# Sparse attention and mLSTM layer: all eight heads' probabilities times values in one change of the matrix array's tiling, with six split weight slots instead of seven

## What is computed

```
h = rmsnorm(x) @ w_in           -> a_q a_k a_v a_z i_q i_k i_w b_q b_k b_v b_z b_o b_i b_f g_a g_b
score = sum over 16 index heads of w_i * relu(q_i . k_i / 8);  keep the best 128 admissible keys
logits = q_a . k_a / 8, masked to those keys;  p = softmax(logits)       # 8 heads of 64
o_a    = p @ v_a                                                         # 8 heads of 64
y_a    = (o_a * silu(a_z)) @ w_branch_a
y_b    = (head_norm(sigmoid(b_o) * mlstm(silu(conv(b_q, b_k)), b_v, gates)) * silu(b_z)) @ w_branch_b
out    = rmsnorm(x + (sigmoid(g_a) * y_a + sigmoid(g_b) * y_b) @ w_out)
```

## Time and profile before

| | us |
|---|---|
| median of three runs | 511.49 |
| the three runs | 511.46 to 511.62 |
| the profiled execution | 511.43 |
| its span, first to last instruction | 509.7 |
| PE busy | 500.9 |
| DVE busy | 258.7 |
| ACT busy | 236.1 |
| POOL busy | 214.6 |

### The profile page before, as it was taken

The page is one execution under the profiler, slowest core; times in us unless marked ns, Lnnn a source line. Parts: engine busy times, 40 slices in busy tenths (PEclk is TensorE's granted clock), DMA queues, the critical chain, the costliest instruction groups (busy, mean ns, idle before and its releaser), DMA issues.

```text
span 509.7 us, 6792 instructions
## 1 busy us (share of the span) xinstructions
PE 500.9 (98%) x2506; PEld 411.4 (81%) x2506; DVE 258.7 (51%) x568; ACT 236.1 (46%) x417; POOL 214.6 (42%) x142
## 2 busy tenths in 40 slices
PE   8999999999999999999999999999999999999995
PEld 7688888888888878888777877888888888887885
DVE  3875778877999915515555557551110011125433
ACT  6756754655533443464577563333321333142322
POOL 1675231333344453256487433056435653373000
PEclk9999999999999999999999999999999999999999
DMA  8653531222243432112121121142244326444111
GB/s 285 200 140 121 140 96 53 84 83 53 74 123 83 120 108 83 42 43 83 44 81 46 47 76 42 42 123 73 56 121 123 107 59 206 125 134 155 41 52 74
DMA packets 44842, 48.94 MB, mean 96 GB/s; under 512 B 4997, under 2 KB 30213, under 8 KB 44809
## 3 DMA queue, kind: packets, MB, share of 16 engines
q1 hardware_dynamic: 43944, 47.65, 32.0%
q10 hardware_dynamic: 864, 0.86, 0.5%
HBM read 46.40 MB, written 2.11 MB: 95 GB/s over the span
## 4 chain that ended last, share of the span: by engine, by line
PE 94%; DMA 2%; SPq 1%; POOL 1%; ACT 1%; DVE 1%; issue 1%; DVEq 0%
PE pj L1423 24%; PE pj L1425 23%; PE pj L1424 23%; PE ob L1533 2%; PE tr L1524 2%; DMA w_raw<-in_w_in 2%; PE ob L1504 2%; PE qb L1494 2%; PE qb L1489 2%; PE qb L1488 2%; PE ob L1424 1%; PE qb L1424 1%; PE ob L1425 1%; PE qb L1425 1%; PE ob L1423 1%; PE qb L1423 1%
## 5 line engine op out<-in xcount | busy, mean ns | idle before, releaser
L513 POOL TENSOR_TENSOR w_lo<-w_raw,w_hi 128x1024 fp32r<-128x1024 f32 x70 | 168.8, 2421 | 144.5 <-ACT w_hi L856 144.4
L1423 PE MATMUL pj<-w_hi,h_hi 128*128 128x512 f32 x272 | 112.8, 415 | 0.0
L1425 PE MATMUL pj<-w_hi,h_lo 128*128 128x512 f32 x272 | 106.5, 392 | 0.0
L1424 PE MATMUL pj<-w_lo,h_hi 128*128 128x512 f32 x272 | 106.5, 391 | 0.0
L1423 PE MATMUL pj<-h_hi,w_hi 128*128 128x512 f32 (+1 forms) x200 | 78.1, 390 | 1.0 <-DVE h_lo L1086 1.0
L856 ACT ACTIVATE w_hi<-w_raw 128x1024 fp32r<-128x1024 f32 (+1 forms) x72 | 73.5, 1045 | 10.2 <-DMA w_raw<-in_w_out 6.4
L1425 PE MATMUL pj<-h_hi,w_lo 128*128 128x512 f32 (+1 forms) x200 | 77.9, 389 | 0.0
L1424 PE MATMUL pj<-h_lo,w_hi 128*128 128x512 f32 (+1 forms) x200 | 77.9, 389 | 0.0
L1425 PEld LDWEIGHTS pj<-w_hi,h_lo 128*128 128x128 f32 x272 | 51.0, 188 | 11.4
L1423 PEld LDWEIGHTS pj<-w_hi,h_hi 128*128 128x128 f32 x272 | 51.2, 188 | 9.7 <-issue 1.1
L1424 PEld LDWEIGHTS pj<-w_lo,h_hi 128*128 128x128 f32 x272 | 51.3, 188 | 9.4 <-issue 1.0
(11 more groups left out here) (201 smaller groups left out, 817.6 us busy)
## 6 DMA issues: line engine op xcount, KB each, us to landing
w_raw<-in_w_in SPq DMA_DIRECT2D x60, 512.0 KB, 3.6
w_raw<-in_w_out SPq DMA_DIRECT2D x5, 512.0 KB, 3.7
x_tok<-in_x SPq DMA_DIRECT2D x4, 512.0 KB, 5.0
w_raw<-in_w_branch_a SPq DMA_DIRECT2D x8, 256.0 KB, 3.0
w_raw<-in_w_branch_b SPq DMA_DIRECT2D x8, 256.0 KB, 3.3
x_again<-in_x SPq DMA_DIRECT2D x1, 2048.0 KB, 10.4
w_late<-in_w_out SPq DMA_DIRECT2D x3, 512.0 KB, 7.3
out<-y_norm SPq DMA_DIRECT2D x4, 320.0 KB, 2.5
```

The source lines that it names most:

```text
L513: eng.tensor_tensor(lo[:, 0:m], raw_slot(n)[:, 0:m], hi[:, 0:m].bitcast(F32), ALU.subtract).then_inc(lo_by_dve if n in DVE_SLOTS else lo_b ...
L1423: pe.matmul(bank, a_hi, b_hi, start=first, stop=False)
L1424: pe.matmul(bank, a_hi, b_lo, start=False, stop=False)
L1425: return pe.matmul(bank, a_lo, b_hi, start=False, stop=last)
```

## The change

`pv_a` is now done once for each token tile, for all eight heads in a row, at attention places 10, 18, 26 and 34, which are the places where the last two heads of each tile were done before. That takes transposed probabilities of eight heads instead of two, in two pieces of four heads (`probs_t0`, `probs_t1`). Their space comes from the weight ring, `SPLIT` 6 instead of 7, and from `gated`, which moves to the zone of the queries `q_a`. With six places the third slot of the next group can no longer be made before the last unit, so `unit_slots` makes the third and the fourth both behind quarter 1 of the last unit. Three of the last eight slots go to places of their own (`EXTRA`) instead of one. `q_a` gets another layout, so that its tiles are contiguous.

```diff
-SPLIT = 7
+EXTRA = (LAST_PLACE, OUT0 + 3, OUT0 + 7)
+SPLIT = 6
...
-        if p >= 4 and p % 2 == 0:
-            put(q, "pv_a", p // 2 - 2)
+        if p >= 6 and p % A_HEADS == 2:
+            put(q, "pv_a", p // A_HEADS - 1)
...
+        z_p = zone(8192)
...
-        q_a = at("q_a", [P, KW, SEQ], F32, z_e)
+        q_a = at("q_a", [P, TILES, KW, P], F32, z_e)
...
-        probs_t = at("probs_t", [P, 2, SEQ], F32, z_h + 4096)
-        gated = at("gated", [P, 2, WIDTH], F32, z_h + 8192)
+        probs_t = [at(f"probs_t{n}", [P, A_HEADS // 2, SEQ], F32, place) for n, place in enumerate((z_h + 4096, z_p))]
+        gated = at("gated", [P, 2, WIDTH], F32, z_e)
...
-            if n == LAST_PLACE:
-                return SPLIT
-            return (n - OUT0 + GATE0 + 6 - (n > LAST_PLACE)) % SPLIT
+            if n in EXTRA:
+                return SPLIT + EXTRA.index(n)
+            return (n - OUT0 + GATE0 - (n > EXTRA[1])) % SPLIT
...
             if g in ("iq0", "iq1"):
-                return {3: [n, n + 1], 2: [n + 2], 1: [n + 3]}[j]
+                return {3: [n, n + 1], 2: [], 1: [n + 2, n + 3]}[j]
             if g == "az":
-                return [n + j] if j < 3 else []
-            return [n + j]
+                return ([n], [n + 1], [], [n + 2])[j]
+            return ([n], [n + 1], [], [n + 2, n + 3])[j]
...
-            return 1 if u + 1 < len(UNITS) and UNITS[u + 1][0] != UNITS[u][0] else -1
+            return 1 if u + 1 == len(UNITS) or UNITS[u + 1][0] != UNITS[u][0] else -1
...
-                    if s >= 2:
-                        wait_full(dve, ("pv_a", s // 2 - 1))
-                    dve.tensor_copy(probs_t[:, s % 2, 0:w], bank_of(job)[:, 0:w]).then_inc(probs_t_made, 1)
+                    if s >= A_HEADS:
+                        wait_full(dve, ("pv_a", s // A_HEADS - 1))
+                    dve.tensor_copy(turned(s % A_HEADS)[:, 0:w], bank_of(job)[:, 0:w]).then_inc(probs_t_made, 1)
...
-                    wait_read(pe, ("probs_chan", s + 1))
-                    b = h // 2
-                    for j in range(i + 1):
-                        for e in range(2):
+                    wait_read(pe, ("probs_chan", s + A_HEADS - 1))
+                    for d in range(0, A_HEADS, 2):
+                        b = (h + d) // 2
+                        for j in range(i + 1):
+                            for e in range(2):
```

More of the change, by code:

```diff
@@ L176, in fills @@
         ring = RING_OF[job[0]]
-        if job[0] == "pv_a" and ATTN[2 * job[1]][1]:
+        if job[0] == "pv_a" and ATTN[A_HEADS * job[1]][1]:
             bank[job] = bank[("pv_a", job[1] - 1)]
@@ L362, in hybrid_kernel @@
         final_row = at("final_row", [P, D_MODEL], F32, z_a + 8192)
-        w_last = [at("w_last_hi", [P, SLOT], F32R, z_f), at("w_last_lo", [P, SLOT], F32R, z_f + 4096)]
+        w_extra = [[at(f"w_extra{n}_{part}", [P, SLOT], F32R, place + size) for part, size in (("hi", 0), ("lo", 4096))]
+                   for n, place in enumerate((z_f, z_p, z_e))]
         y_tok = at("y_tok", [P, 2, D_MODEL], F32, z_hlo)
@@ L573, in wait_unit_read, with turned @@
                 eng.wait_ge(unit_out, u + 1)
+        def turned(head):
+            return probs_t[head // (A_HEADS // 2)][:, head % (A_HEADS // 2), :]
         def wait_slot_used(eng, n):
@@ L745, in side @@
                         hi = q_twice[same, i % 2, e, :, :]
-                        pool.tensor_tensor(q_lo[same, i % 2, e, :, :], q_a[same, :, i * P:(i + 1) * P],
+                        pool.tensor_tensor(q_lo[same, i % 2, e, :, :], q_a[same, i, :, :],
                                            hi.bitcast(F32), ALU.subtract).then_inc(q_lo_made, 1)
@@ L884, in job_side @@
                     wait_full(act, job)
[L885 removed]
+                    act.activation(q_a[:, j, :, :],
                                    bank_of(job)[:, :].rearrange("p (b t) -> p b t", t=P), ACT.Copy)\
@@ L981, in split_queries @@
                     same = slice(e * A_DIM, (e + 1) * A_DIM)
-                    act.activation(q_twice[same, i % 2, e, :, :], q_a[same, :, i * P:(i + 1) * P], ACT.Copy)\
+                    act.activation(q_twice[same, i % 2, e, :, :], q_a[same, i, :, :], ACT.Copy)\
                         .then_inc(q_hi_made, 1)
@@ L985, in split_queries @@
                     same, other = slice(e * A_DIM, (e + 1) * A_DIM), slice((1 - e) * A_DIM, (2 - e) * A_DIM)
-                    act.activation(q_twice[other, i % 2, e, :, :], q_a[same, :, i * P:(i + 1) * P], ACT.Copy)\
+                    act.activation(q_twice[other, i % 2, e, :, :], q_a[same, i, :, :], ACT.Copy)\
                         .then_inc(q_doubled, 1)
@@ L1525, in side @@
                 elif kind == "pv_a":
[L1526 removed]
+                    s = A_HEADS * job[1]
                     i, h = ATTN[s]
[L1528 to L1535 removed]
+                    wait_read(pe, ("probs_chan", s + A_HEADS - 1))
[3 more added lines that the diff above has]
+                            for e in range(2):
+                                same = slice(e * A_DIM, (e + 1) * A_DIM)
+                                head = h + d + e
+                                ins = pe.matmul(bank[same, b * P:(b + 1) * P], v_a[:, j, head * A_DIM:(head + 1) * A_DIM],
+                                                turned(head)[:, j * P:(j + 1) * P], start=(j == 0), stop=(j == i),
+                                                tile_position=(0, e * A_DIM))
                 elif kind in ("out_a_chan", "out_b_chan"):
```

13 lines of the change are left out of this document (4 added, 9 removed).

## The result

| | before | after |
|---|---|---|
| median | 511.57 us, 14 runs (511.38 to 511.68) | **513.46 us**, 14 runs (511.86 to 515.33) |
| ratio | | **1.0034**, 95% interval 1.0020 to 1.0048 |
| span of the profiled execution | 509.7 us | 511.7 us |

I had predicted 508.4 and a range up to 509.5. The kernel after lies 5.1 us above the forecast. Its runs also spread as those of before don't: five between 511.9 and 512.3 at a mean granted clock of 0.998 to 0.999, six between 513.2 and 513.6 at 0.995, three between 515.0 and 515.3 at 0.991. The run that was profiled is one of the middle six.

The account below looks back on a forecast made before the run. PE bounds the kernel, busy 98% of the span. 511.43 - 3.6 (blocks' fixed cost) - 0.14 (wait at place 30) + 0.7 (wait at step 13) = 508.4 us, range 507.5 to 509.5.

Parts of the forecast that it names:

- The block's fixed cost: Each pv_a block in the attention costs PE 0.30 us beyond its records; twelve of sixteen blocks lose it, 3.6 us saved.
- step 13: At attention step 13 PE's transposes wait for an exponential whose time comes from POOL's chain: 0.7 us lost, bounds 0.4 to 1.0.
- 3.6 + 0.14: Attention gains: 3.6 us of fixed block cost, and 0.14 us for PE's wait at place 30 on DVE's copy of turned probabilities.
- The slope: Each record in a pv_a block costs PE 0.056 us, taken to hold also in blocks of 32 to 64 records.
- Six slots: In the weight ring, later remainders of moved slots cost zero, cover 1.25 us; ACT's second rounding zero, bound 0.3 us.
- the covers of slots 20, 24 and 28: Time from remainder's end to PE's use: 1.25 us left for slot 20, 1.95 for 24; 28 repeats 24.
- My rival of a slower kernel: In quarter 3 of a group's first unit, the ring of six stalls PE at the fourth slot: 514.0 us, chance 0.04.
- no other new idle time of PE above 0.1: Sign in the profile after: beyond about 0.7 us ahead of one attention transpose, PE gains no idle time above 0.1.
- From group av back everything at the old time on PE within 0.1 us: Sign in the profile after: PE's times from group av back stay as before the change, within 0.1 us.

Follow-up runs that it names:

- e1_early7: The kernel after with slots 7 and 8 put in other places and rounded at their old, earlier time; 508.95 us, ratio 0.9948.
- e4_rows_psum: The kernel after, all slots late, with only DVE's running maximum of the gate rows moved to a free PSUM bank; 508.85 us, ratio 0.9949.
- e7_root_psum: e4_rows_psum with POOL's root chain ahead of slot 41's remainder; 508.75 us, ratio 0.9946.
- e10_late7_swap: The kernel before, ring of seven, slot 7 rounded late with slot 8, two places exchanged so that slot 8 waits for slot 2; 511.89 us, ratio 1.0007.
- e6_early7_root: e1_early7 with POOL's root chain ahead of slot 41's remainder; 508.87 us, ratio 0.9949.
- e9_gated_first: e7_root_psum with slot 41's remainder moved behind POOL's first gated tile, to the start of bz's second unit; 507.84 us, ratio 0.9927.
- e3_ring_only: The kernel before with the ring of six, moved tiles and changed roundings, but pv_a still for two heads at a time; 516.4 us, ratio 1.0094.
- e11_late7_shift: The kernel before, ring of seven, slot 7 rounded late, slot 7 in slot 1's place and slot 8 in slot 2's; 517.76 us, ratio 1.0101.

## Why the prediction was wrong

**The block's fixed cost: right.** The steps of the attention without the one at step 13 sum to -2.72 - 0.96 = -3.68, where I had 3.6 + 0.14 = 3.74. The slope holds up to 64 records. The timeline of PE after, the last block; the earlier trace rows answer to it:

```profile
317.63 0.40 PE L1431 MATMUL pj<-w_hi,h_lo 128*128 128x512 f32 x1
317.96 3.71 PE L1541 MATMUL ob<-probs_t,v_a 128*64 128x128 f32 x64
321.60 0.50 PE L1429 MATMUL pj<-w_hi,h_hi 128*128 128x512 f32 x1
```

Between its neighbours 3.97, of which 0.23 would be there without it: 3.74. The 64 records start 0.0546 apart (3.44 for 63 steps), which leaves 0.25 for the fixed part. I had said 3.9, with 0.056 and 0.30.

**Step 13: right in kind, mis-sized.** I had 0.7 and a start of POOL's chain 0.39 before the old 257.77.

```profile
262.15 0.30 POOL L777 TENSOR_SCALAR b_rstd<-mean_var 128x16 f32<-128x16 f32 x1
...
267.49 1.65 ACT L1001 ACTIVATE cell<-cell,b_mean_neg,b_rstd 128x128 f32<-128x128 f32 x4 [1.40 <-POOL b_mean_neg L786]
...
270.73 0.41 PE L1530 MATMUL tr<-ident,probs 128*128 128x128 f32 x2 [0.77 <-ACT probs L929]
```

262.15 less the 4.76 is 257.39, as forecast. The wait cost 0.96 (0.93 in e1_early7 and e4_rows_psum), inside the bounds of 0.4 to 1.0, near the end that the hand-over and the exposed weight load were to add. Together with the blocks the net gain was 2.6 to 2.7 us, where I had 3.0.

**Six slots: the step that failed.** I put it at zero with 0.3 as the bound, by the covers of slots 20, 24 and 28. These came out as said: the remainders end 1.28, 1.99 and 1.99 us ahead of their use, where I had 1.25 and 1.95. But a cover asks only whether the moved work is in time for whoever needs it. I never asked what else runs where the work lands. The remainders of slots 7 and 8 end 4.4 and 2.8 us ahead of their use where nothing delays PE (e7_root_psum), and after they cost 3.1 us of wait and, in the profiled run, 1.5 of lower clock. My rival of a slower kernel had the same edit and the wrong place: it looked for a late remainder at a group's start, while the loss is a remainder in time that stands in the way of another engine. That its 514.0 lies near the measured 513.46 is luck.

The hint stood in the trace of before: two scans of the same shape on DVE, one of 1.21 us and one of 1.84. Both overlap POOL's remainder of 34.24. The first reads one operand from PSUM (`tr`), the slow one reads only `a_row`, in SBUF. That the slow one takes 1.21 when no remainder is running at its start only e10_late7_swap showed.

**The signs I had named.** Two of them point at the failed step: "no other new idle time of PE above 0.1", where 2.9 stands at `stage`, and "From group av back everything at the old time on PE within 0.1 us", where PE is 4.7 late.

## What to carry to other kernels

What follows holds for the forms measured here. When a change moves work on one engine, lay the new times beside every engine that shares something with it, not only beside its consumers. Where GpSimd works in SBUF, a short VectorE instruction that reads SBUF twice or is a plain SBUF-to-SBUF step can last until GpSimd's is over, and one PSUM operand freed it. Compare instructions of the same form: one that takes longer than its twin may already be waiting. And reordering work within a full stretch of an engine only handed the wait to the next consumer (e6_early7_root, e7_root_psum); it went when something left that stretch (e9_gated_first).

## What the runs showed of the hardware that I had not expected

- A 4x512 negation and a 4x512 two-operand step were lengthened from 0.42 to 2.45 us and from 0.68 to 2.81 by a GpSimd subtraction of 128x1024. With one PSUM operand both took 0.68 beside the same subtraction.
- It isn't a matter of four partitions. The kernel before has such holds on 128 of them as well: DVE's `oa_lo`, 128x512 with both inputs in SBUF, takes 0.68 at its shortest and 2.91 and 2.60 beside POOL. By the last row below, 339.03 - 0.68 = 338.35, and POOL's records end at 338.48.

```profile
330.62 7.86 POOL L513 TENSOR_TENSOR w_lo<-w_raw,w_hi 128x1024 fp32r<-128x1024 f32 x3 [12.52 <-ACT w_hi L856]
...
330.96 2.91 DVE L1282 TENSOR_TENSOR oa_lo<-o_at,oa_hi 128x512 fp32r<-128x512 f32 x1
...
336.43 2.60 DVE L1282 TENSOR_TENSOR oa_lo<-o_at,oa_hi 128x512 fp32r<-128x512 f32 x1 [0.77 <-ACT oa_hi L930]
```

- The profile shows the held time as busy time of DVE, and POOL's held time as busy of POOL (5.68 and 5.15 for two remainders that take 4.75 freely). No view names it as a wait: DVE's busy time rose by 4.0 us with not one instruction more.
- A gap of PE of 3.1 us cost 1.5 us more behind it, at the 1.2 GHz level, in the profiled run of the kernel after. The runs of the kernel after, of e3_ring_only and of e11_late7_shift all spread upwards from their best as the mean clock falls from 0.999 to 0.991; those without the gap spread by 0.5 us at the most. In e11_late7_shift's profiled run the same gap is followed by wide matmuls 0.43 apart until 51.8, and 6.2 us are lost, 3.0 of them behind the gap. The length of the slow stretch differs from run to run; what decides it stays open.
- Why a hold ends 0.14 us before POOL's record does was not tried; both ends are what the profile makes of them.
